# A second attention whose value products start on activations that are not normalised yet

## The reference

```python
xn = rms_norm_2(h, norm_g)                 # h * rsqrt(mean(h*h over the width) + EPS) * norm_g
proj = xn @ w_in                           # 1024 -> q 1024, k 1024, v 1024, 8 forget gates
...
q_fox = rms_norm_2(q[:, :H_FOX], fox_q_g)  # a norm over each head's 64 columns; k and the other
...                                        # kind of heads alike
o_fox = forgetting_attention(q_fox, k_fox, v[:, :H_FOX], log_f)
o_sb = stick_breaking_attention(q_sb, k_sb, v[:, H_FOX:])
...
return o @ w_out
```

## Time and profile before

| | |
|---|---|
| median of 3 runs | 1254.68 us (1254.67 to 1256.55) |
| profiled execution | 1254.08 us, of which the span of the trace is 1252.3 us |
| busy in the span | TensorE 1236.1 us (99%), its weight load 1093.4, DVE 724.3, POOL 713.0, ACT 679.3 |
| granted TensorE clock | 1.000 over the span, 1.00 in each of the 40 slices |
| DMA | 208.09 MB, 166 GB/s on average |

### The profile page before, as it was taken

The page is one execution under the profiler, slowest core; times in us unless marked ns, Lnnn a source line. Parts: engine busy times, 40 slices in busy tenths (PEclk is TensorE's granted clock), DMA queues, the critical chain, the costliest instruction groups (busy, mean ns, idle before and its releaser), DMA issues.

```text
span 1252.3 us, 23640 instructions
## 1 busy us (share of the span) xinstructions
PE 1236.1 (99%) x8381; PEld 1093.4 (87%) x8381; DVE 724.3 (58%) x1574; ACT 679.3 (54%) x1232; POOL 713.0 (57%) x308
## 2 busy tenths in 40 slices
PE   8999999999999999999999999999999999999998
PEld 5788889877799899999988879999999999999998
DVE  5696667446522555555615663766666324766665
ACT  6342334455544666666645636666667545666663
POOL 5476553442258555557495406655575986655563
PEclk9999999999999999999999999999999999999999
DMA  8978541222145455546364203545554654554451
GB/s 327 371 256 311 194 159 69 87 99 58 46 127 179 133 166 187 199 168 228 119 183 155 84 18 111 191 168 186 200 204 135 200 186 140 181 201 172 180 215 54
DMA packets 58187, 208.09 MB, mean 166 GB/s; under 512 B 6640, under 2 KB 7808, under 8 KB 58112
## 3 DMA queue, kind: packets, MB, share of 16 engines
q1 hardware_dynamic: 57888, 206.56, 48.6%
q0 software_dynamic: 224, 0.52, 0.1%
HBM read 206.01 MB, written 1.05 MB: 165 GB/s over the span
## 4 chain that ended last, share of the span: by engine, by line
PE 91%; DVE 4%; ACT 2%; POOL 1%; DMA 1%; issue 1%; SPq 0%; DVEq 0%; ACTq 0%
PE ps L555 18%; PE ps L526 15%; PE ps L527 15%; PE ps L528 15%; PE ps L557 9%; PE ps L813 2%; PE ps L580 2%; PE ps L582 2%; PE ps L583 2%; PE ps L610 1%; PE ps L884 1%; PE ps L910 1%; PE ps L899 1%; POOL wlo L333 1%; ACT whi L1272 1%
## 5 line engine op out<-in xcount | busy, mean ns | idle before, releaser
L333 POOL TENSOR_TENSOR wlo<-raw,whi 128x1024 fp32r<-128x1024 f32 x287 | 696.4, 2440 | 509.8 <-ACT whi L1272 486.7
L1272 ACT ACTIVATE whi<-raw 128x1024 fp32r<-128x1024 f32 x338 | 352.6, 1053 | 75.4 <-DMA raw<-in_stream 37.3
L555 PE MATMUL ps<-H,whi 128*128 128x512 f32 x1024 | 365.1, 399 | 1.4 <-DVE H L1814 1.2
L557 PE MATMUL ps<-H,wlo 128*128 128x256 f32 x1024 | 287.6, 281 | 0.0
L526 PE MATMUL ps<-H,whi 128*128 128x256 f32 (+2 forms) x960 | 285.7, 298 | 0.8 <-POOL wlo L333 0.4
L527 PE MATMUL ps<-H,whi 128*128 128x256 f32 (+2 forms) x960 | 277.4, 289 | 0.0
L528 PE MATMUL ps<-H,wlo 128*128 128x256 f32 (+2 forms) x960 | 277.4, 289 | 0.0
L555 PEld LDWEIGHTS ps<-H,whi 128*128 128x128 f32 x1024 | 192.5, 188 | 48.5 <-DVE H L1814 3.3
L526 PEld LDWEIGHTS ps<-H,whi 128*128 128x128 f32 (+1 forms) x960 | 183.3, 191 | 13.4 <-issue 8.8
L557 PEld LDWEIGHTS ps<-H,wlo 128*128 128x128 f32 x1024 | 193.5, 189 | 0.0
L2179 DVE SCALAR_TENSOR_TENSOR arena<-ps,sm,arena 128x255 f32<-128x255 f32 (+1 forms) x264 | 127.4, 483 | 103.6 <-ACT arena L1541 96.4
(11 more groups left out here) (330 smaller groups left out, 1484.7 us busy)
## 6 DMA issues: line engine op xcount, KB each, us to landing
raw<-in_stream SPq DMA_DIRECT2D x386, 512.0 KB, 4.1
X<-in_xc SPq DMA_DIRECT2D x4, 512.0 KB, 6.0
out_y<-X SPq DMA_DIRECT2D x8, 128.0 KB, 1.9
kx<-in_const SPq DMA_DIRECT2D x1, 512.0 KB, 8.6
params<-in_params SPq DMA_DIRECT2D x1, 344.0 KB, 7.3
kx<-in_const POOLq DMA_DIRECT2D x1, 256.0 KB, 4.5
k<-in_const POOLq DMA_DIRECT2D x1, 129.0 KB, 5.6
k<-in_const SPq DMA_DIRECT2D x1, 128.0 KB, 5.6
```

Of the source, the lines that this page charges most:

```text
L333: pool.tensor_tensor(wlo[:, slot, :], raw[:, rslot, :], whi[:, slot, :].bitcast(f32), ALU.subtract).then_inc(rest_done[0], 1)
L555: pe.matmul(PS[:, bank, :], wh_, F[:, k, :, :].rearrange("p h n -> p (h n)"), start=k == 0, stop=False, skip_group_check=True)
L557: mm = pe.matmul(PS[:, bank, T:2 * T], wl_, Fh[:, k, :], start=False, stop=k == KC - 1, skip_group_check=True)
L1272: act.activation(whi[:, s % RING, :], raw[:, r % RING, :], ACT.Copy).then_inc(hi_done, 1)
```

## The change

It has four parts.

1. The value products use `Vh` and `Vl`, halves of X times the norm's weight, but not divided by the rms. DVE and ACT make them between the additions to X. The rms is a factor of each token, that is of each row of the value result, so the copy out of PSUM multiplies each row by it (`rcol`). Two products of 1/rms with a column of the identity turn it onto the partitions.
2. The scaled activations `Fh` and `Fl`, which the projections still need, are made beside the value products, through PSUM banks 1 to 3 in place of `h32`. The values therefore go to banks 4 to 7, and projections 0 and 1 to banks 2 and 3.
3. `keep_running` ahead of the values goes. The sums of squares move behind the first value block. POOL waits for the last `Vl` before it makes the low half of the third value block.
4. ACT's set-up of the head rows moves behind the value products (it writes the tiles that now hold `Vh` and `Vl`), and the seven set-up operations of DVE move into the loop over the projections, behind the copy of projection 0.

```diff
@@ pool
+                    if s == S_ATT2 + 2:
+                        pool.wait_ge(S["vl_done"], KC)
@@ names
+        Vh, Vl = Gh, Gl
+        rcol = SM[:, 288:290]
+        def q_bank(j):
+            return 2 + j if j < 2 else 4 + j % 2
@@ tensor
-            sumsq(2)
-            keep_running(S_ATT2, 31)
...
             for k in range(KC):
                 wait_rest(pe, S_ATT2 + k)
-                product_n(S_ATT2 + k, D, k, lambda half: [(tt, (PS[:, 2 * tt + half, :], True)) for tt in range(2)],
-                          norm=2)
+                pe.wait_ge(S["vl_done"], k + 1)
+                product_n(S_ATT2 + k, D, k, lambda half: [(tt, (PS[:, 4 + 2 * tt + half, :], True)) for tt in range(2)],
+                          Vh, Vl)
+                if k == 0:
+                    sumsq(2)
+                if k == 5:
+                    pe.wait_ge(S["newton"], 3)
+                    for tt in range(2):
+                        mm = pe.matmul(PS[:, 0, tt:tt + 1], n_r[:, P * tt:P * tt + P], ident[:, 0:1],
+                                       start=True, stop=True)
+                    mm.then_inc(S["rc_ps"], 1)
             def project(j):
+                if j == 0:
+                    pe.wait_ge(S["hl_done"], HU[2] + KC)
...
             def forget_gates():
                 pe.wait_ge(S["wg_lo"], 2)
+                pe.wait_ge(S["evac_v"], v_before + 4)
@@ scalar
-            norm(2)
+            act.preload_act_table_set("natural_log_exp_and_others")
+            for k in range(KC):
+                act.wait_ge(S["x_ready"], 8 + k + 1)
+                act.activation(Vh[:, k, :], X[:, k, 0:T], ACT.Copy, scale=pr("anorm", k, k + 1)).then_inc(S["vh_done"], 1)
+                act.activation(sq[:, k, 0:T], X[:, k, 0:T], ACT.Square).then_inc(S["sq_ready"], 1)
+            splits_upto(S_ATT2 + RING)
+            rsqrt_start(2)
+            for u in range(KC):
+                act.wait_ge(S["h32_done"], HU[2] + u + 1)
+                act.activation(Fh[:, u, :], PS[:, 1 + u % 3, 0:T], ACT.Copy).then_inc(S["hh_done"], 1)
+                if u % 2 == 1:
+                    splits_upto(S_ATT2 + RING + u // 2)
...
+            splits_upto(S_ATT2 + KC + RING - 2)
+            act.wait_ge(blk_done, S_ATT2 + KC)
             for out in (*head_rows, *spread2):
...
-            for k in range(KC):
-                splits_upto(S_ATT2 + k + RING)
+            splits_upto(S_ATT2 + KC + RING - 1)
@@ vector
-            add_to_x(2, S_ATT2 - 1, lambda k: MODB[:, 24 + k:25 + k])
+            for k in range(KC + 1):
+                if k < KC:
+                    wait_sums(2, S_ATT2 - 1, k)
+                    dve.scalar_tensor_tensor(X[:, k, 0:T], PS[:, k // 2, (k % 2) * T:(k % 2) * T + T],
+                                             MODB[:, 24 + k:25 + k], X[:, k, 0:T], ALU.mult, ALU.add)\
+                       .then_inc(S["x_ready"], 1)
+                if k >= 1:
+                    dve.wait_ge(S["x_ready"], 8 + k)
+                    dve.wait_ge(S["vh_done"], k)
+                    dve.scalar_tensor_tensor(Vl[:, k - 1, :], X[:, k - 1, 0:T], pr("anorm", k - 1, k),
+                                             Vh[:, k - 1, :].bitcast(f32), ALU.mult, ALU.subtract)\
+                       .then_inc(S["vl_done"], 1)
...
-            norm(2, lambda u: pr("anorm", u, u + 1))
+            dve.wait_ge(S["ss_ready"], 3)
+            newton(n_v[:, 0:T], PS[:, 1, 0:T], n_t[:, 0:T], n_r[:, 0:T], ss_out(2),
+                   1.0 / D, S["newton"], lambda x: dve.wait_ge(S["y0_done"], 4 + x))
+            dve.wait_ge(S["newton"], 3)
+            for u in range(KC + 1):
+                if u < KC:
+                    if u >= 3:
+                        dve.wait_ge(S["hl_done"], HU[2] + u - 2)
+                    dve.scalar_tensor_tensor(PS[:, 1 + u % 3, 0:T], X[:, u, 0:T], pr("anorm", u, u + 1), n_r[:, 0:T],
+                                             ALU.mult, ALU.mult).then_inc(S["h32_done"], 1)
+                if u >= 1:
+                    dve.wait_ge(S["hh_done"], HU[2] + u)
+                    dve.tensor_tensor(Fl[:, u - 1, :], PS[:, 1 + (u - 1) % 3, 0:T], Fh[:, u - 1, :].bitcast(f32),
+                                      ALU.subtract).then_inc(S["hl_done"], 1)
...
-            for bank in range(4):
-                dve.tensor_copy(v2[:, bank // 2, 512 * (bank % 2):512 * (bank % 2) + 512], PS[:, bank, :])\
-                   .then_inc(S["evac_v"], 1)
+            for n in range(4):
+                dve.tensor_scalar(v2[:, n // 2, 512 * (n % 2):512 * (n % 2) + 512], PS[:, 4 + n, :],
+                                  rcol[:, n // 2:n // 2 + 1], None, ALU.mult).then_inc(S["evac_v"], 1)
...
                 if j < 16:
                     dve.wait_ge(S["qk_sq"], 10 + j + 1)
-                    dve.tensor_copy(q2[:, j, :], PS[:, 4 + j % 2, 0:T]).then_inc(S["evac_v"], 1)
+                    dve.tensor_copy(q2[:, j, :], PS[:, q_bank(j), 0:T]).then_inc(S["evac_v"], 1)
...
+                if j == 0:
+                    link(dve.tensor_scalar(selr, K0[:, 0:8], 0.0, None, ALU.mult))
...
```

More of the change, by code:

```diff
@@ L564, in product_halves, with product_n @@
                     sumsq(norm, KC - 2, KC)
-            def product_n(s, width, k0, at, norm=None):
+            def product_n(s, width, k0, at, hi=Hh, lo=Hl):
                 for c in range(D // width):
                     k = k0 + c
-                    if norm is not None:
-                        pe.wait_ge(S["hl_done"], HU[norm] + k + 1)
                     wide = min(width, 512)
@@ L1650, in _ @@
                         act.wait_ge(S["st_done"], 10 + j - 1)
-                    act.activation(sqr2[j % 2], PS[:, 4 + j % 2, 0:T], ACT.Square).then_inc(S["qk_sq"], 1)
+                    act.activation(sqr2[j % 2], PS[:, q_bank(j), 0:T], ACT.Square).then_inc(S["qk_sq"], 1)
                     if j in (5, 9, 13):
@@ L2235, in finish_qk @@
                                          ALU.mult, ALU.mult).then_inc(S["qk_fin"], 1)
-            link(dve.tensor_scalar(selr, K0[:, 0:8], 0.0, None, ALU.mult))
-            link(dve.tensor_copy(selr[0:8, :], ident[0:8, 0:8]))
-            link(dve.tensor_copy(selr[32:40, :], ident[32:40, 32:40]))
-            link(dve.tensor_copy(identr, ident))
-            link(dve.tensor_copy(maskr, maskA))
-            for rows_r in (cfk, cfq):
-                link(dve.tensor_scalar(rows_r, K0[:, 0:T], 0.0, None, ALU.mult))
             def forget_part(n):
@@ L2321, in fox_turned @@
                 dve.tensor_copy(f_PT[h % 4], PS[:, 4 + h % 2, 0:3 * P]).then_inc(S["fox_pt"], 1)
+            dve.wait_ge(S["rc_ps"], 1)
+            dve.tensor_copy(rcol, PS[:, 0, 0:2]).then_inc(S["rc_done"], 1)
+            dve.wait_ge(S["rc_done"], 1)
             dve.wait_ge(blk_done, S_ATT2 + KC)
-            for bank in range(4):
-                dve.tensor_copy(v2[:, bank // 2, 512 * (bank % 2):512 * (bank % 2) + 512], PS[:, bank, :])\
-                   .then_inc(S["evac_v"], 1)
+            for n in range(4):
+                dve.tensor_scalar(v2[:, n // 2, 512 * (n % 2):512 * (n % 2) + 512], PS[:, 4 + n, :],
+                                  rcol[:, n // 2:n // 2 + 1], None, ALU.mult).then_inc(S["evac_v"], 1)
             for j in range(18):
@@ L2350, in _ @@
                     forget_part(j - 5)
+                if j == 0:
+                    link(dve.tensor_scalar(selr, K0[:, 0:8], 0.0, None, ALU.mult))
+                    link(dve.tensor_copy(selr[0:8, :], ident[0:8, 0:8]))
+                    link(dve.tensor_copy(selr[32:40, :], ident[32:40, 32:40]))
+                    link(dve.tensor_copy(identr, ident))
+                    link(dve.tensor_copy(maskr, maskA))
+                    for rows_r in (cfk, cfq):
+                        link(dve.tensor_scalar(rows_r, K0[:, 0:T], 0.0, None, ALU.mult))
                 if j == 3:
```

9 lines of the change are left out of this document (4 added, 5 removed).

## The result

The changed kernel takes 1258.14 us (median of 19 runs, 1257.29 to 1268.43), the kernel before 1255.04 us (19 runs, 1254.09 to 1257.92) beside it. The ratio is 1.0034, 95% interval 1.0021 to 1.0047: slower by 0.2 to 0.5%. The forecast was 1260.2 us. The profiled execution's span is 1255.9 us, 3.6 above that of before, where 5.5 were forecast.

What follows compares the result with a forecast made beforehand. TensorE's own queue was taken to bound the kernel (91% of the chain of waits). Terms −4.5 + 8.3 + 1.7 = +5.5 us on 1254.08 give 1259.6, plus 0.6 for the median: 1260.2 us, range 1252 to 1264.

Steps and rivals of the forecast that it cites:

- Gain ahead of the projections: TensorE before the second attention's projections: 4.8 us removed, 0.5 added, projections starting at 637.4 instead of 641.95; gain 4.5 us.
- b0: First of the attention's 24 weight blocks (b0 to b7 values, b8 onward projections); forecast to start at 611.7 us.
- Inputs in time: Start of the value products: first halves ready at 609.7, low halves all near 615.1; no wait, cost 0.
- POOL beside the norm: Norm's chunks on DVE: 0 to 2, 6 and 7 wait for POOL, 3 to 5 pass; last low half at 637.1.
- cost 0: Norm's last low half at 637.1, TensorE wanting it at 637.4: no cost, 0.3 us to spare.
- POOL is left behind: POOL's low halves after the norm run late: b10 ends 642.4, b11 644.8, b12 647.2.
- POOL: continuous from 615: Sign to look for in POOL's timeline: it works without a break from 615 us.
- Set-up operations: DVE's seven behind projection 0's copy: five wait for POOL subtractions, second copy done 658.3, TensorE stalls 8.3 us.
- One operation passes at the end of each: DVE's set-up beside POOL's subtractions: operations pass at 647.2, 649.6, 652.1, 654.5, 657.0, the last two at once.
- Clock behind the stall: TensorE after its pause near 650 us: slower clock costs 1.7 us, bounds 0 and 1.7.
- the operations pass cheaply: Rival: DVE's set-up slips through POOL's gaps, or POOL idles at 646; −4.5 us, 1250.2 us; chance 0.17.
- The norm was not last: Rival: all eight norm chunks wait for POOL, first projection 6 us late; 1256 to 1261 us; chance 0.06.

Runs made afterwards that it cites:

- e2_spread: Changed kernel with one of the seven DVE set-up operations behind each of the first seven projection copies: 1250.93 us, ratio to before 0.9980.
- e6_psum_rms: Changed kernel with the norm's chunk products reading the reciprocal roots from PSUM, chunks through two banks instead of three: 1251.96 us, ratio to before 0.9970.
- e3_pool_waits: Changed kernel with POOL waiting, ahead of its subtraction of b13, until the seven set-up operations are done: 1251.73 us, ratio to before 0.9972.
- e5_three: Changed kernel with three set-up operations left behind the first copy, the other four one each behind the third to sixth: 1253.69 us, ratio to before 0.9978.
- e9_nine: Changed kernel with the last two set-up operations done twice, nine in all behind the first copy: 1260.81 us, ratio to before 1.0044.
- e7_on_act: Changed kernel with all seven set-up operations made by ACT behind the head rows, none by DVE: 1252.81 us, ratio to before 0.9971.
- e8_spread_psum: Changed kernel with the edits of e2_spread and e6_psum_rms joined: 1251.64 us, ratio to before 0.9962.
- e4_warm: Changed kernel with 50 unread TensorE products of 256 columns ahead of the fourth projection's wait: 1260.70 us, ratio to before 1.0035.
- e11_warm44: Changed kernel with 44 unread TensorE products of 256 columns ahead of the fourth projection's wait: 1259.00 us, ratio to before 1.0026.
- e10_no_waits: Changed kernel with five set-up operations issued without waits between them, then one wait, the two dependent ones, one wait: 1259.31 us, ratio to before 1.0030.
- e12_act_psum: Changed kernel with the edits of e7_on_act and e6_psum_rms joined: 1252.35 us, ratio to before 0.9970.

## Why the prediction was right, and where it was not

- **Gain ahead of the projections: 4.5 forecast, 4.34 measured.** b0 at 611.88 (forecast 611.7), the two new products 0.50 us long as assumed, projections at 637.61 (forecast 637.4). The two ways to this term did not quite agree: 4.8 less 0.5 is 4.3, the sum by blocks gives 4.5. e2_spread, where nothing takes it back, shows a gain of 3.7 in the span and about 4 between full-clock runs.
- **Inputs in time: right.** No wait ahead of b0 or b1.
- **POOL beside the norm: right in kind.** Chunks 0 to 2, 6 and 7 were held, 3 to 5 passed, as written. The last low half came at 636.2 for 637.1. The step "cost 0" was true for TensorE there, and incomplete: the held chunks delay the splits, POOL stands idle for 2.46 and 1.74 us, and its work is left over for the stage behind. The forecast carried that backlog ("POOL is left behind") and never asked what it was worth; e6_psum_rms shows 5.3 us of the pause. The sign "POOL: continuous from 615" left these two gaps out, although the working had them both.
- **Set-up operations: right in kind, mis-sized.** "One operation passes at the end of each" subtraction, five slow and two fast, is what the rows show, and e3_pool_waits, e5_three and e9_nine confirm it. The term of the sum that was off is the stall, 8.3 forecast and 6.4 measured. The 1.9 between them are four parts. The first operation ended, with b12, at 646.3 and not at 647.2, since POOL began its last run at 636.74 and not 637.6, with the norm ending earlier: 0.9. A subtraction took 2.35 us and not 2.45: 0.5 over four of them. The last operations and the copy took 0.2 less. The copy was wanted at 650.4 and not 650.1: 0.3.
- **Clock behind the stall: 1.7 forecast, 1.6 measured.** 86.11 − 78.13 − 6.40 = 1.58. The 16 products at 0.21 us where 0.12 is usual give (0.213 − 0.12) × 16 = 1.5, and the two kernels with filled pauses came 1.4 lower. The price had come from the only cold stretch of the trace, the start of the program, and was the upper of two bounds. That a pause in mid-program costs about the same was not to be read from the trace of before; the closeness of the figure is in part luck.
- **The sum:** −4.34 + 6.40 + 1.58 = 3.64, the 3.6 of the spans. The forecast of 5.5 lies 1.9 us above it, which is the stall; the medians differ by 3.1 us.
- **The rivals.** That the operations pass cheaply hung on whether POOL had finished b15 before the third was up; it finished b15 about 653.2, the third was up at 648.6. The norm was not last, by 1.4 us. The short stall did not come here, but it is what e5_three and e6_psum_rms are: 1.1 us of pause, and no half clock behind it.

## What to carry to other kernels

When a change starts one engine's queue earlier, look at which chains of small operations of another engine it now runs beside. Where one of the two holds up the other, as POOL's subtractions did DVE's set-up here, a chain costs about (number of operations) × (length of the other's instruction) for as long as the other has work queued, whatever the operations' own size. Spread such a chain over the waits of its engine, or give it to an engine that isn't held (ACT in e7_on_act). A product with two SBUF inputs can read one of them from PSUM (e6_psum_rms). And an operation that is held without cost where it stands may still delay the engine behind it, and so leave work over for a later stage. Ask what the other engine would have done in its idle time.

## What the runs showed that I had not expected

- The clock also falls where no long pause is, and not in every execution. In the profiled executions of e5_three, e7_on_act, e8_spread_psum, e4_warm and e11_warm44 a half clock began between 728 and 738 us, each time 0.9 to 3.1 us behind the begin of a pause of 0.76 us that all kernels have there, the one before too; in those of before, the changed kernel, e2_spread, e3_pool_waits, e6_psum_rms, e9_nine, e10_no_waits and e12_act_psum none did, with the same 0.76 us. Other stretches at half clock came earlier in the program in seven of the thirteen. By the clocks of the runs, half-clock stretches are the largest part of the spread between runs: e2_spread took 1249.95 to 1250.42 us in six runs at a full clock and 1254.72 to 1256.94 in five at 0.995 or 0.996. The changed kernel never had a full clock in 19 runs (0.997 at best); its own pause alone gives 0.997, as the profiled execution shows. Where the clock fell in the runs that were not profiled isn't known. What decides whether the clock falls there stays open.
- A pause of 1.1 us cost hardly more than itself (e5_three and e6_psum_rms, 79.31 − 78.13 = 1.18 us in all), one of 6.3 to 7.1 us halved the clock each time (changed, e9_nine, e10_no_waits). Nothing in between was run.
- One copy of 0.43 us into PSUM, which lets the norm's products through beside POOL, took 5.3 us off the pause.
